# A lag of three steps from scores to transposes, and scores of two query blocks together, in a four-branch attention trunk

## What is computed

```python
h = layer_norm(h, ln0_g, ln0_b)
for l in range(2):
    p = split_cols(h @ w_in[l])
    a = causal_dense_attention(p.a_q, p.a_k, p.a_v, decay=cumsum(log_sigmoid(p.a_f + b_f)))   # A
    b = mla_attention(p.b_cq, p.b_ckv, p.b_kr, w_uq, w_ukv)     # B: latent q and kv, rotary part of 32
    c = dsa_sparse_attention(p.c_q, p.c_k, p.c_v, p.c_iq, p.c_ik, p.c_iw, top_k=256)          # C
    d = sliding_window_sink_attention(p.d_q, p.d_k, p.d_v, window=128, sinks)                 # D
    mixed = concat(a * silu(p.a_g), b * silu(p.b_g), c * silu(p.c_g), d * silu(p.d_g))
    h = layer_norm(ALPHA * h + mixed @ w_out[l], ln_g[l], ln_b[l])
```

## Time and profile before

| | |
|---|---|
| median of 3 runs | 2946.27 us (2945.33 to 2946.93) |
| the profiled execution | 2943.56 us, span 2941.6 us, mean granted clock 0.994 |
| PE, PEld busy | 97%, 57% |
| DVE, ACT, POOL busy | 55%, 36%, 22% |
| DMA | 154.36 MB on the hardware queue, 16.4% of the 16 engines' span |

### The profile page before, as it was taken

How to read it: one execution, slowest core, us unless ns; L and a number is a source line. 1 busy time by engine, 2 the same in 40 slices (tenths; PEclk the granted TensorE clock), 3 DMA queues, 4 the chain that set the end, 5 groups by cost and what they waited for, 6 DMA issues and landing times. The chain is left out here.

```text
span 2941.6 us, 39580 instructions
## 1 busy us (share of the span) xinstructions
PE 2854.4 (97%) x13638; PEld 1675.1 (57%) x13638; DVE 1621.2 (55%) x4361; ACT 1059.6 (36%) x3085; POOL 642.6 (22%) x1336
## 2 busy tenths in 40 slices
PE   7999999999999999999999999999999999999998
PEld 5446666555566666644544466665555666665443
DVE  5337888767776433322333388886767764323232
ACT  3334444343455345500012334443334544445000
POOL 1002333111122244500000022331112222444000
PEclk9999999999999999999999999999999999999999
DMA  6201111111110121042120011111011101201421
GB/s 225 66 8 47 44 44 33 38 33 45 37 32 19 33 99 33 26 149 79 58 91 31 10 45 44 44 33 45 28 43 37 33 17 33 106 28 30 155 86 43
DMA packets 90908, 156.88 MB, mean 53 GB/s; under 512 B 11296, under 2 KB 67248, under 8 KB 88920
## 3 DMA queue, kind: packets, MB, share of 16 engines
q1 hardware_dynamic: 90712, 154.36, 16.4%
HBM read 120.13 MB, written 32.08 MB: 52 GB/s over the span
## 5 line engine op out<-in xcount | busy, mean ns | idle before, releaser
L1160 PE MATMUL ps_s<-xT,w_ring 128*128 128x348 f32 (+4 forms) x3616 | 1122.4, 464 | 12.6 <-DVE gate L1617 5.0
L1160 PEld LDWEIGHTS ps_s<-xT,w_ring 128*128 128x128 f32 x3616 | 673.3, 191 | 396.4 <-issue 102.6
L1412 ACT ACTIVATE arena<-ps_t 16x32 f32<-16x32 f32 (+3 forms) x1048 | 367.2, 373 | 239.9 <-PE ps_t L1230 225.7
L1399 ACT ACTIVATE arena<-arena,small 128x1040 f32<-128x1040 f32 (+8 forms) x544 | 372.0, 684 | 132.4 <-DVE small L1679 131.6
L1442 DVE MAX8 small<-score 128x8 f32<-128x1040 f32 (+6 forms) x448 | 376.3, 840 | 10.5
L1444 DVE MATCH_REPLACE8 score<-small,score 128x1040 f32<-128x1040 f32 (+6 forms) x448 | 370.0, 826 | 0.0
L1230 PE MATMUL ps_t<-ident,arena 128*128 128x128 f32 (+1 forms) x2016 | 300.5, 278 | 13.0 <-ACT arena L1412 12.9
L1791 POOL TENSOR_SCALAR strips<-arena,small 128x16 f32<-128x16 f32 x384 | 107.1, 279 | 902.2 <-DVE small L1691 902.2
L1203 PE MATMUL ps_s<-feat 64*128 64x272 f32 (+12 forms) x1680 | 295.6, 454 | 3.3 <-ACT arena L1315 3.2
L1230 PEld LDWEIGHTS ps_t<-ident,arena 128*128 128x128 f32 (+1 forms) x2016 | 224.2, 140 | 116.6 <-issue 67.0
L1794 POOL TENSOR_SCALAR arena<-arena,small 128x1024 f32<-128x1024 f32 (+7 forms) x384 | 286.2, 745 | 0.0
(11 more groups left out here) (177 smaller groups left out, 2504.8 us busy)
## 6 DMA issues: line engine op xcount, KB each, us to landing
w_ring<-in_w_feat SPq DMA_DIRECT2D x78, 512.0 KB, 3.5
mixed<-mixg SPq DMA_DIRECT2D x128, 128.0 KB, 1.7
feat<-mixed SPq DMA_DIRECT2D x16, 1024.0 KB, 6.7
resid<-score SPq DMA_DIRECT2D x16, 512.0 KB, 3.2
score<-resid SPq DMA_DIRECT2D x16, 512.0 KB, 7.6
arena<-in_w_out SPq DMA_DIRECT2D x4, 1536.0 KB, 8.0
cT<-falls SPq DMA_DIRECT2D x8, 520.0 KB, 4.8
feat<-falls SPq DMA_DIRECT2D x8, 520.0 KB, 5.2
```

The lines of the kernel that those rows point to most:

```text
L1160: mm = pe.matmul(ps_s[:, bank, 0:w], w_ring[:, wt % 2, k, :], xT[:, k, c0:c0 + w], start=(k == 0), stop=(k == KT - 1))
L1399: nc.scalar.activation(p, p, ACT.Exp, scale=-1.0, bias=nm[:, e:e + 1], accum_out=psums[0:M, st % 4, e:e + 1]).then_inc(S["exp_done"], 1)
L1412: a = nc.scalar.activation(dst, src, ACT.Copy)
```

## The change

`LAG` becomes 3. A pair is cut into rounds (`rounds_of`); the scores of all blocks of a round are issued together, then the round's steps follow with their `tp`, `exp`, `top` and `fill` as before. In D's first three pairs two blocks make a round, and there the reciprocals of the round before come ahead of the scores. In B and C blocks 3, 2 and 1, 0 make a round. `probs` gets a fourth row, and two small blocks can share one (`row_of`). The chunks are dealt out anew: G at steps 0, 1 and 3 (4 in D's first three pairs), Q at 2, 3, 5 in D and from 2, 4, 5 on elsewhere; C's chunks are cut in halves of the contraction that lie in nine steps. In B the blocks up to 3 have one score product where they had two. The scaling of `cn` is an item of its own (`cs`), ahead of the token blocks, and the last two latents of the layer move behind the G chunk of step 0 in D's last pair. The number of selection operations in D's last pair is smaller at steps 5 to 8.

In the opening, the second to ninth block in order are normalised in place in `x_in` by ScalarE, with a bias that POOL makes by two more operations, and the wait for the store of `x_new` is gone; TensorE starts with 20 transposes of the identity, ScalarE with a small activation; VectorE's constants move behind the opening. A chunk of the index projection waits for the copies of its own tokens only.

```diff
-LAG = 2
+LAG = 3
 ORDER = [8, 7, 6, 5, 4, 3, 2, 1, 0]
-ROW_AT, ROW_LEN = [0, 1040, 1952], 2736
+ROW_AT, ROW_LEN = [0, 1040, 1952, 2736], 3392
...
-TOP_RATE = {"A": [3, 4, 5, 5, 6, 4, 5, 5, 1], "D": [4, 4, 4, 4, 4, 4, 4, 4, 4],
-            "B": [4, 4, 5, 5, 5, 5, 5, 4, 1], "C": [0] * 9}
+TOP_RATE = {"A": [3, 4, 5, 5, 6, 4, 5, 5, 2], "D": [4, 4, 4, 4, 4, 4, 4, 4, 4], "D3": [4, 4, 4, 4, 4, 3, 2, 3, 3],
+            "B": [4, 4, 5, 5, 5, 5, 5, 4, 2], "C": [0] * 9}
+def top_rate(br, p):
+    return TOP_RATE["D3" if br == "D" and p == NP - 1 else br]
...
+def rounds_of(br, p):
+    if br == "D" and p < NP - 1:
+        return [[8, 7], [6, 5], [4, 3], [2, 1], [0]]
+    if br in "BC":
+        return [[8], [7], [6], [5], [4], [3, 2], [1, 0]]
+    return [[i] for i in ORDER]
+def row_of(br, p, i):
+    if br == "D" and p < NP - 1:
+        t = len(rounds_of(br, p)) * p + (NB - 1 - i) // 2
+        return (t + 1) % 4, 2 * BLK * ((NB - 1 - i) % 2)
+    if i == 2 and br in "BC":
+        return 1, keys_of(3)
+    return ((NB - 1 - i) % 4, 0) if i else (3, keys_of(1))
...
-        products = even(n, 2 if n >= 272 else 1)
+        products = even(n, 2 if i > 3 else 1)
...
+    def halves(self, l, what, **kw):
+        out, wt = [], self.open()
+        for c in (2, 1, 0) if what == "G" else range(3):
+            begun = {}
+            out.append(lambda c=c, begun=begun: begun.update(self.chunk(l, wt, what, c, k1=KT // 2, **kw)))
+            out.append(lambda begun=begun: self.add(**dict(begun, k0=KT // 2, k1=KT)))
+        return out
...
-        for idx, work in enumerate(self.tile(l, "G", br=br, p=p)):
+        late = 4 if br == "D" and p < NP - 1 else 3
+        for idx, work in zip((0, 1, late), self.tile(l, "G", br=br, p=p) if br != "C" else []):
             put(idx, work)
         if br == "A":
             if p + 1 < NP:
                 rest = self.tile(l, "AQ", p=p + 1) + self.tile(l, "AK", p=p + 1)
             else:
                 rest = self.tile(l, "K", br="D") + self.tile(l, "Q", br="D", p=0)
-            for idx, work in zip((3, 4, 5, 6, 7, 7), rest):
+            for idx, work in zip((2, 4, 5, 6, 7, 7), rest):
...
-                for idx, work in zip((3, 4, 5), self.tile(l, "Q", br="D", p=p + 1)):
+                for idx, work in zip((2, 3, 5), self.tile(l, "Q", br="D", p=p + 1)):
                     put(idx, work)
                 for idx, b in zip((6, 7, 8), range(3 * p, 3 * p + 3)):
+                    if b:
+                        put(idx, lambda b=b: self.scale(l, b if b == NB - 1 else b - 1))
                     if b == NB - 2:
                         put(idx, lambda: self.token_block(l, "TB", NB - 1, bank=self.free_bank()))
                     if b < NB - 1:
                         put(idx, lambda b=b: self.token_block(l, "TB", b))
-                    if b:
-                        put(idx, lambda b=b: self.latent(l, b if b == NB - 1 else b - 1))
+                        if b:
+                            put(idx, lambda b=b: self.latent(l, b - 1))
...
-                put(0, lambda: self.latent(l, NB - 2))
+                fill[0].insert(0, lambda: self.scale(l, NB - 2))
+                for b in (NB - 1, NB - 2):
+                    put(0, lambda b=b: self.latent(l, b))
...
+            rest = self.halves(l, "G", br=br, p=p) + self.halves(l, "Q", br="C", p=p + 1)
+            for idx, work in zip((0, 0, 1, 1, 2, 3, 4, 5, 6, 7, 7, 8), rest):
                 put(idx, work)
         else:
+            for idx, work in zip((0, 0, 1, 1, 2, 3), self.halves(l, "G", br=br, p=p)):
...
+        for blocks in rounds_of(br, p):
+            if l == DEPTH - 1 and 0 in blocks:
+                blocks = blocks[:-1]
+            steps = [self.step(l, br, p, i, hu) for i in blocks]
+            if len(steps) > 1 and br == "D":
+                self.normalise()
+            for s in steps:
+                if br == "A":
+                    self.add("tri", **s)
+                if br == "C":
+                    self.add("near", **s)
+            if steps:
+                self.add("qk", l=l, br=br, p=p, idx=steps[0]["idx"], hu=hu, steps=steps, ready=steps[0]["ready"])
+                self.normalise()
+                self.values()
+            self.pending += steps
+            for s in steps:
+                if early and s["idx"] == NB - 1:
+                    early()
+                old = self.pending.pop(0) if len(self.pending) > LAG else None
+                if self.pv_next and old and old["i"] == 0:
+                    self.values()
+                self.probabilities(old, 0)
+                self.add("exp", e=0, **s)
+                self.gated()
+                self.add("top", l=l, count=top_rate(br, p)[s["idx"]])
+                work = fill.get(s["idx"], [])
+                between = 0 if br == "D" else 1
+                for fn in work[:between]:
+                    fn()
+                self.probabilities(old, 1)
+                self.add("exp", e=1, **s)
+                for fn in work[between:]:
+                    fn()
+            self.rec_next += steps
+        if l == DEPTH - 1:
+            self.empty_step(l, br, p, early, fill.get(NB - 1, []))
...
+        def normed(n, M):
+            return x_in[n][0:M, :] if n < NB else x_new[0:M, n % 2, :]
...
+            for _ in range(20):
+                pe.transpose(ps_t[:, 0, 0:BLK], ident[:], ident[:])
...
-                        all_left(pe, it["upto"]["tg"])
-                    waits(pe, it["free"])
...
+                elif kind == "ln" and 0 < it["ln"] < NB:
+                    ln, M, r = it["ln"], rows_of(it["b"]), it["ln"] % 2
+                    act.wait_ge(S["ln_rs"], ln + 1)
+                    nc.scalar.activation(x_in[ln][0:M, :], x_in[ln][0:M, :], ACT.Identity, scale=rstd[0:M, r, 0:1],
+                                         bias=rstd[0:M, r, 1:2]).then_inc(S["ln_act"], 1)
...
-                elif kind == "ct":
+                elif kind == "cs":
```

More of the change, by code:

```diff
@@ L287, in latent, with scale, chunk @@
         self.ct_end = self.n["tg"]
+    def scale(self, l, b):
+        self.add("cs", l=l, b=b, cn=self.cn_of[(l, b)])
     def open(self):
         return self.take("wt")
-    def chunk(self, l, wt, what, c, bank=P_BANK, **kw):
+    def chunk(self, l, wt, what, c, bank=P_BANK, k1=KT, **kw):
         pieces = IQ_CHUNKS if what == "IQ" else (CHUNKS if what in ("IK", "AK", "K") else asked(l))
@@ L534, in empty_step @@
+    def empty_step(self, l, br, p, early, work):
         self.normalise()
@@ L785, in build @@
         for it in items:
-            if it["kind"] == "mt" and it["what"] == "G":
+            if it["kind"] == "mt" and it["what"] == "G" and it["k1"] == KT:
                 at = it["nth"]
@@ L1284, in _ @@
                     act.wait_ge(S["consts"], 16 * 7)
+                elif kind == "iw" and l == 0:
+                    for j in range(2):
+                        act.wait_ge(x_st[j], 16 * len([n for n in range(NB) if n % 2 == j]))
+                elif kind == "ln" and 0 < it["ln"] < NB:
[3 more added lines that the diff above has]
+                                         bias=rstd[0:M, r, 1:2]).then_inc(S["ln_act"], 1)
                 elif kind == "xt":
@@ L1527, in _ @@
+                    if ln >= NB + 2:
+                        dve.wait_ge(x_st[r], 16 * len([n for n in range(ln - 1) if n % 2 == r]))
                         if it["xprev"]:
```

286 lines of the change are left out of this document (143 added, 143 removed).

## The result

The changed kernel takes 2953.5 us (median of 12 runs, 2950.3 to 2956.6), the kernel before 2945.1 beside it (12 runs). The ratio is 1.0029, 95% interval 1.0021 to 1.0037: slower by 0.3%, where 1.1% faster was forecast. The profiled execution took 2956.6 us, its span is 2954.8.

A forecast was written before the change was run, and what follows sets the result against it. TensorE, with a matmul in 97% of the span, was taken as the bound. Terms -18.5 + 14.8 - 14.0 - 5.0 - 8.7 + 4.5 - 5.0 = -31.9 us took 2946.27 to 2914 us, range 2896 to 2934.

The forecast's parts named there:

- (8): Booked at nothing: the lag itself, the moved weight loads, two divisions ahead of D's scores, the moved chunks of A.
- (1): Fewer rounds of scores, 24 in D's first three pairs, 12 each in B and C: gain 18.5 us.
- Waits for VectorE in A: In A: listed, without a size, among the signs that would show the forecast wrong.
- (6): Merged blocks 3, 2 without a chunk at step 6, B pairs 1, 2 and C pair 3: cost 4.5 us, bounds 0 and 10.
- (2): D's merged rounds uncover waits for the chunks' PSUM bank at 22 places: cost 14.8 us, bounds 0 and 31.
- (3): Separate scaling of cn and later latent transposes remove the wait for VectorE: gain 14.0 us, bounds 8 and 15.3.
- (4): D's last pair: the values product's wait of 3.05 and 3.16 us and slow product shrink: gain 5.0, bounds 1 and 9.
- (5): C's gate and Q chunks in halves over nine steps remove pair-end waits and slow stretches: gain 8.7 us.
- (7): The opening: normalising in place on ScalarE removes VectorE's pace and the store wait: gain 5 us, bounds 2 and 9.
- Rival four: Opening: warm-up transposes don't count as busy, first blocks stay at 1.2 GHz, 2.5 us lost; chance 0.35 beside any other.
- Rival three: D: each of 22 new bank waits pulls the clock to 1.2 GHz, 56 us in all, so 2970; chance 0.05.

The follow-up runs named there:

- lag3_single: The changed kernel with one query block a round everywhere, lag of three kept: 2947.5 us.
- lag2: The changed kernel with one query block a round everywhere and LAG back to 2: 2911.0 us, ratio 0.9887 to the kernel before.
- before_gate3: The kernel before, with A's third gate chunk at step 3 and the first of the other six at step 2: 2938.7 us, ratio 0.9982.
- d_single: The changed kernel with D's first three pairs back to one query block a round: 2950.9 us.
- no_warm: The changed kernel without the 20 transposes ahead of the first block: 2953.8 us.
- combined: The changed kernel with the last chunk of A's pairs and B's last at step 8, A's selection operations redistributed, a second bank in D's merged rounds: 2907.5 us.
- best_plain: The kernel of combined with one query block a round in B and C: 2902.7 us, ratio 0.9859 to the kernel before.
- bc_single: The changed kernel with B and C back to one query block a round: 2948.6 us.

## Why the prediction was wrong

The sum said -31.9 us for the profiled execution; it became +13.1 (by the medians +8.4, since the profiled execution of the changed kernel was its slowest). By its steps, the step between A0 and C3 taken as above:

**(8), booked at nothing, is the step that failed: "the lag itself" and "the moved chunks of A".** A and C3 grew by 31.7 us in the trace, 28.3 without the work that only moved, and one constant undoes 36.5 (lag3_single, lag2). The moved chunks alone cost nothing (before_gate3). I looked at whom the lag helps, the block that waits for POOL, and not at what it shifts: the values products go from even to odd steps, block 3's three groups of transposes from a step with a chunk between them to one without. Both were cover for another engine. Step (1) even uses the shift, for the rounds of D, B and C, and I did not ask what it does in A. The rows to see it with were there: the chunk behind a gate chunk starts 1.36 us after that one's end, with no more than scores and transposes between the earlier trace rows, so behind five selection operations it starts later still. I costed where each chunk went, but not what stood between it and the next user of its bank. "Waits for VectorE in A" stood among the signs of a wrong forecast, and no rival had it.

**(1) and (6), merging in B and C, have the wrong sign.** The forecast for them was a gain of 10.1 less 4.5, 5.6 us; single rounds won 4.9. The saved change of mode is real where nothing else is in the way (in D, with the second bank, merged rounds beat single ones by 2.9 and 3.1 us for 12 rounds less), but in the round of blocks 3 and 2 the scores had covered a copy, at every pair and not only at the six places of (6).

**(1) and (2) in D were right.** Waits of 0.92, 0.37 and 1.33 stand where the prediction put them; 8.4 saved and 14.8 paid make 6.4 lost, and d_single gave back 5.3 in these pairs. The second bank, which took 11.4 of the 14.8 away, shows that cost from the other side.

**(3) and (4), forecast 19.0:** with single rounds and a lag of two D is 15.9 us shorter, where apart from these two steps and the places of two chunks nothing in it changed. Right in kind, 3 too high. The slow product of the earlier trace rows wasn't there in before_gate3, the same code in D: D's last pair in layer 1 was 3.7 shorter without any edit. Part of (4) is chance.

**(5), forecast 8.7:** pairs 0 to 2 of C gave 7.2 with merged rounds, 9.5 with single ones (lag3_single). Right. The two slow stretches of the earlier trace rows are in this too; before_gate3 lacks both without an edit, 1.5 us each in C2.

**(7), forecast 5.0:** 3.2 in the profiled run, 2.3 to 6.7 in the other kernels with this opening. Right, with a spread of its own. Rival four was half right: the warm-up changes nothing in the end, but for another reason than the one it gave.

Rival three, the only one on the slow side, had the right mechanism in the wrong stage: a wait for a bank that pulls the clock down. In D the new waits of 0.37 to 1.33 us did not; in A those of 2.3 to 2.8 did, in some executions.

The steps account for nearly all of the 45.0 us between -31.9 and +13.1: 31.7 of (8), 10.5 of (1) and (6) in B and C, 3.1 of (3) and (4) and 1.8 of (7), less 0.8 of (5), about 1 of (1) and (2) in D, and 1.1 by which the two output projections got shorter, make 44.

## What to carry to other kernels

A lag between stages in an order written out by hand is a shift of everything that the later stages do against everything in the earlier steps. So before it is changed, list for each shared buffer what stands between two users of it, before and after, with the third engine's queue at that point; a short score or product that looks like mere work may be the cover of a copy. And when a change of many parts disappoints, run the one that was booked at nothing by itself first.

## What the runs showed of the hardware

Transposes alone raised TensorE's level, as the durations show. In each of the 12 kernels with the 20 transposes ahead they took 0.19 to 0.23 us apiece, and the 8 behind them 1.04 to 1.87 us; without them (before, before_gate3, no_warm) the first 8 took 1.94. Where the level outlasted the wait behind (as in combined, lag2 and best_plain), the next 8 took 1.07 and the first 16 matmuls 2.13 us in place of the changed kernel's 4.05. By the Trainium skill, "TensorE: Matmul & The Clock Gate", Part 4 (PE-mode transpose), the full clock doesn't engage for transposes, since they don't count as TensorE being busy in the same way as matmuls do. The fp32 transposes of these traces contradict it.

A wait of 2.3 to 2.8 us for a bank can cost more than itself, but it is not certain. In A0 of layer 0 the same wait of 2.32 us stands before the same 16 matmuls; in the changed kernel they take 4.75 us to the next start (granted clock 1.00), and in bc_single 6.44 (0.52 in the slow stretch of it, 269.2 to 272.6):

```profile
270.62 4.92 PE L1233 MATMUL ps_s<-xT,w_ring 128*128 128x348 f32 x16 [2.32 <-DVE gate L1734]
```

```profile
268.79 6.61 PE L1231 MATMUL ps_s<-xT,w_ring 128*128 128x348 f32 x16 [2.32 <-DVE gate L1732]
```

In A1 it is the other way round: behind the wait before 346.23 they take 6.45 us in the changed kernel, and this pair is 1.7 us shorter in bc_single, no_warm and lag3_single; d_single is slow in both pairs. A difference of 1.7 us between two single traces is therefore no sign of an edit.
